# An expert layer's weight tiles in a new order, with the 32 extra tokens multiplied over two up-matrices at once

## The reference

```python
# x: 256 tokens x 1024. 8 experts, hidden size 3584, top 2 experts for each token
logits = h @ w_router + b_router            # 256 x 8
gate   = softmax over each token's 2 best experts
for e in experts:
    y += gate[:, e] * ((silu(h @ moe_w1[e]) * (h @ moe_w3[e])) @ moe_w2[e])
x = x + gt2 * y
```

## Time and profile before

| | us |
|---|---|
| median of 3 runs | 3112.54 (3109.74 to 3120.24) |
| the profiled execution's own time | 3107.25 |
| its span, first to last instruction | 3105.5 |
| PE busy in the span | 2710.2 (87%) |
| DVE busy | 1233.1 (40%) |
| ACT busy | 575.5 (19%) |
| mean granted clock of TensorE | 0.924 of full speed |

### The profile page before, as it was taken

One profiled execution on the slowest core, in us unless ns is written; L12 is line 12 of the kernel. 1 busy time (PEld: TensorE's weight loads), 2 busy tenths in 40 slices (PEclk: granted clock), 3 DMA queues, 4 the chain that ended last, 5 costly groups with the idle time before them and its releaser, 6 DMA issues.

```text
span 3105.5 us, 35726 instructions
## 1 busy us (share of the span) xinstructions
PE 2710.2 (87%) x14339; PEld 1731.7 (56%) x14339; DVE 1233.1 (40%) x1834; ACT 575.5 (19%) x905; POOL 281.0 (9%) x332
## 2 busy tenths in 40 slices
PE   5987999898678878879989989899899987668998
PEld 2754658754434434436767767574468653224883
DVE  2204235663401001006656656530245549981111
ACT  1101420001100000005535545400111010001110
POOL 1100410000000000000000000000000074650000
PEclk8997769999799999999989989999999997668999
DMA  7421728992399999997747657644258730003441
GB/s 282 97 80 53 205 82 300 324 338 100 112 394 394 394 395 393 394 396 268 256 172 255 221 201 259 218 136 149 81 190 293 275 135 28 0 0 115 149 150 67
DMA packets 315342, 648.45 MB, mean 209 GB/s; under 512 B 12450, under 2 KB 102765, under 8 KB 311040
## 3 DMA queue, kind: packets, MB, share of 16 engines
q10 hardware_dynamic: 151440, 358.68, 31.8%
q1 hardware_dynamic: 158544, 272.84, 25.5%
q0 software_dynamic: 5216, 14.96, 2.2%
HBM read 645.38 MB, written 1.05 MB: 208 GB/s over the span
## 4 chain that ended last, share of the span: by engine, by line
PE 64%; DMA 16%; DVE 12%; issue 3%; ACTq 2%; POOL 1%; ACT 1%; DVEq 0%; POOLq 0%
PE bank L1347 16%; DMA ring<-in_moe_w 11%; PE bank L1363 11%; PE bank L573 5%; PE bank L575 4%; PE bank L574 4%; PE bank L1589 4%; DMA arena<-in_w_ada 3%; PE bank L588 3%; DVE arena L1915 3%; ACTq L444 2%; PE bank L1675 2%; DVE arena L1924 2%; PE bank L533 1%; PE bank L585 1%
## 5 line engine op out<-in xcount | busy, mean ns | idle before, releaser
L1347 PE MATMUL bank<-HT,ring 128*128 128x256 f32 x2816 | 625.8, 386 | 19.0 <-DVE arena L1915 13.6
L1347 PEld LDWEIGHTS bank<-HT,ring 128*128 128x128 f32 x2816 | 544.8, 194 | 99.7 <-DVE arena L1915 15.7
L925 DVE TENSOR_TENSOR w_low<-ring,w_high 128x1024 fp32r<-128x1024 f32 x252 | 305.4, 1224 | 127.9 <-ACT w_high L731 125.7
L1363 PE MATMUL bank<-ring,arena 128*128 128x512 f32 x784 | 339.8, 595 | 0.7 <-ACT arena L1101 0.7
L731 ACT ACTIVATE w_high<-ring 128x1024 fp32r<-128x1024 f32 x252 | 265.3, 1059 | 195.4 <-PE bank L575 193.7
L1924 DVE SCALAR_TENSOR_TENSOR arena<-arena,small 128x512 f32<-128x512 f32 x288 | 216.6, 752 | 143.9 <-DMA arena<-in_ada_w 89.9
L1363 PEld LDWEIGHTS bank<-ring,arena 128*128 128x128 f32 x784 | 149.6, 191 | 188.4 <-issue 186.0
L909 DVE TENSOR_TENSOR HT<-HT,bank 128x256 f32<-128x256 f32 x35 | 14.7, 421 | 442.9 <-PE bank L547 425.4
L508 PE MATMUL bank<-ring,arena 128*64 128x256 f32 x1120 | 134.9, 384 | 45.0 <-DMA ring<-in_moe_w 45.0
L547 PE MATMUL bank<-ring,arena 128*64 128x256 f32 x1120 | 135.7, 385 | 43.0 <-DMA ring<-in_moe_w 42.9
L573 PE MATMUL bank<-w_high,tokens_low 128*128 128x512 f32 x336 | 144.1, 429 | 11.3 <-DVE w_low L925 8.5
(11 more groups left out here) (371 smaller groups left out, 3219.5 us busy)
## 6 DMA issues: line engine op xcount, KB each, us to landing
ring<-in_moe_w ACTq DMA_DIRECT2D x340, 1024.0 KB, 13.8
arena<-in_ada_w SPq DMA_DIRECT2D x96, 512.0 KB, 6.0
ring<-in_ffn_w_up SPq DMA_DIRECT2D x44, 1024.0 KB, 5.1
ring<-in_ffn_w SPq DMA_DIRECT2D x33, 1024.0 KB, 6.6
ring<-in_w_ada SPq DMA_DIRECT2D x24, 1024.0 KB, 9.8
arena<-in_w_ada SPq DMA_DIRECT2D x48, 512.0 KB, 5.5
ring<-in_ret_w_in SPq DMA_DIRECT2D x24, 1024.0 KB, 5.2
ring<-in_ffn_w_down SPq DMA_DIRECT2D x22, 1024.0 KB, 5.0
```

Of the source, the lines that this page charges most:

```text
L925: dve.tensor_tensor(out=WL[half % SPLIT][:, :], in0=slot(i)[:, HALF * (half % 2):HALF * (half % 2) + HALF], in1=WH[half % SPLIT][:, :], op ...
L1347: mm = pe.matmul(PS[b][:, SEQ * m:SEQ * m + SEQ], w[:, k, P * m:P * m + P], src[:, k, :], start=k == 0, stop=k == KD - 1)
L1363: mm = pe.matmul(bank(4 + 2 * t + n), lhs(2 * j + k)[:, P * t:P * t + P], w[:, k, BANK * n:BANK * n + BANK], start=j + k == 0, stop=j == t ...
```

## The change

The order of tiles becomes: in step c the tiles w1 h = 0, w3 h = 0, w1 h = 1, w3 h = 1 of chunk c, then both w2 tiles of chunk c - 1; 8 steps in place of 9. AHEAD is 3 in place of 4. PE, ACT and DVE follow that order. The extras of w1 and w3 are done together, once for each h, when both tiles are in the ring: column groups 0 and 1 take w1, groups 2 and 3 take w3, 256 columns each, all into bank 1. Silu of the extras is taken from partitions 0 to 63 and multiplied by partitions 64 to 127. The transposes of chunk c - 1 (4, then 2 of 64 partitions for the extras, before: 1 and 4) stand after the h = 0 part of chunk c. Before step c PE waits for the hidden values of chunk c - 1 (`moe_hid`), since banks 0, 1 and 2 are used again.

```diff
-MOE_STEPS = MOE_CHUNKS + 2
+MOE_STEPS = MOE_CHUNKS + 1
...
-        for name, chunk in (("w1", c), ("w2", c - 2), ("w3", c)):
-            if 0 <= chunk < MOE_CHUNKS:
-                order += [(name, chunk, 0), (name, chunk, 1)]
+        if c < MOE_CHUNKS:
+            order += [(name, c, h) for h in range(2) for name in ("w1", "w3")]
+        if c >= 1:
+            order += [("w2", c - 1, 0), ("w2", c - 1, 1)]
...
-        AHEAD = 4
+        AHEAD = 3
...
+                def extra_up(c, h):
+
+                    w = [cols_of(moe_first + tile_at[kind, c, h], 4) for kind in ("w1", "w3")]
+                    for k in range(4):
                         for n in range(4):
+                            mm = pe.matmul(PS[1][32 * n:32 * n + 32, 0:SEQ], XGX[:, 4 * h + k, :], w[n // 2][:, k, SEQ * (n % 2):SEQ * (n % 2) + SEQ],
+                                           start=h + k == 0, stop=h == 1 and k == 3)
+                    mm.then_inc(sem("tile_used"), 2)
...
+                    for q in range(4):
+                        pe.transpose(PS[7][:, P * q:P * q + P], MS[c % 2][:, P * q:P * q + P], ident[:, :])
+                    for b in range(2):
+                        mm = pe.transpose(PS[3][:, P + 64 * b:P + 64 * b + 64], MSX[c % 2][0:64, P * b:P * b + P], ident[0:64, 0:64])
+                    mm.then_inc(sem("moe_turned"), 1)
...
-                pe.wait_ge(sem("extra_x"), j + 1)
                 for c in range(MOE_STEPS):
+                    if c >= 1:
+                        pe.wait_ge(sem("moe_hid"), g * MOE_CHUNKS + c)
                     if c < MOE_CHUNKS:
-                        if c:
-                            pe.wait_ge(sem("moe_silu"), g * MOE_CHUNKS + c)
-                        tiles("w1", c, 0, 1)
+                        for h in range(2):
+                            for kind, b in (("w1", 0), ("w3", 2)):
+                                product(kind, c, 2 * h, b)
+                                product(kind, c, 2 * h + 1, b)
+                            if c + h == 0:
+                                pe.wait_ge(sem("extra_x"), j + 1)
+                            extra_up(c, h)
+                            if h == 0 and c >= 1:
+                                turn_hidden(c - 1)
                     if c == MOE_CHUNKS:
-                        pe.wait_ge(sem("moe_silu"), g * MOE_CHUNKS + MOE_CHUNKS)
+                        turn_hidden(c - 1)
                         pe.wait_ge(sem("pick_ready"), g + 2)
                         gather()
...
+                    if c >= 1:
+                        pe.wait_ge(sem("hid_low"), j * MOE_CHUNKS + c)
+                        if c == MOE_CHUNKS:
                             turn_gates()
+                        for h in range(2):
+                            product("w2", c - 1, 2 * h, 4)
+                            product("w2", c - 1, 2 * h + 1, 4)
+                            extra_down(c - 1, h)
```

On ACT in a wide round (DVE has the same order, with `hidden_low`, the two products into MS and MSX in place of `silu`, and `begin_round` after the first four halves of step 0):

```diff
                     if c < MOE_CHUNKS:
-                        split("w1", c)
...
+                        split("w1", c, 0, 2)
+                        split("w3", c, 0, 2)
+                        split("w1", c, 2, 4)
+                    if c >= 1:
+                        hidden_high(c - 1)
+                    if c < MOE_CHUNKS:
+                        split("w3", c, 2, 4)
+                    if c >= 1:
+                        split("w2", c - 1)
+                    if c < MOE_CHUNKS:
                         silu(c)
+                    else:
+                        act.wait_ge(sem("gather_done"), g + 2)
+                        tokens_high()
```

More of the change, by code:

```diff
@@ L380, in build @@
         MS = [hidden[:, BANK * i:BANK * (i + 1)] for i in range(2)]
-        MSX = [hidden[:, D + P * i:D + P * (i + 1)] for i in range(2)]
+        MSX = [hidden[:, D + SEQ * i:D + SEQ * (i + 1)] for i in range(2)]
         def in_ad(off, *shape):
@@ L500, in narrow @@
                         if c >= 2:
-                            pe.wait_ge(sem("moe_silu"), g * MOE_CHUNKS + (c - 1))
+                            pe.wait_ge(sem("moe_hid"), g * MOE_CHUNKS + (c - 1))
                         for h in range(2):
[L503 to L509, removed]
@@ L576, in product @@
                     mm.then_inc(sem("w_used"), 1)
-                def extra(kind, c, h, b):
-                    w = cols_of(moe_first + tile_at[kind, c, h], 2 if kind == "w2" else 4)
-                    for k in range(2 if kind == "w2" else 4):
+                def extra_up(c, h):
+                    w = [cols_of(moe_first + tile_at[kind, c, h], 4) for kind in ("w1", "w3")]
+                    for k in range(4):
                         for n in range(4):
[L583 to L589, removed]
-                    mm.then_inc(sem("tile_used"), 1)
@@ new lines, in extra_down @@
+                def extra_down(c, h):
+                    w = cols_of(moe_first + tile_at["w2", c, h], 2)
+                    for k in range(2):
+                        o = 64 * k + 32 * h
+                        for n in range(4):
+                            mm = pe.matmul(PS[6][32 * n:32 * n + 32, 0:SEQ], MHTX[c % 2][:, o:o + 32], w[:, k, SEQ * n:SEQ * n + SEQ],
+                                           start=c + h + k == 0, stop=c == MOE_CHUNKS - 1 and h + k == 2)
+                    mm.then_inc(sem("tile_used"), 1)
@@ L693, in narrow, with loads @@
                 now, after = experts_of(g)
+                def loads(first, used):
+                    for i in range(first, min(used + RING - AHEAD + 1, NT)):
+                        load_ahead(g, now, after, i)
+                    return max(first, used + RING - AHEAD + 1)
                 i = 0
                 for c in range(MOE_STEPS):
-                    until = tile_at["w1", c, 1] if c < MOE_CHUNKS else tile_at["w3", MOE_CHUNKS - 1, 1]
-                    while i <= until + RING - AHEAD:
-                        load_ahead(g, now, after, i)
-                        i += 1
+                    i = loads(i, tile_at["w3", c, 0] if c < MOE_CHUNKS else tile_at["w2", MOE_CHUNKS - 2, 1])
+                    if c >= 1:
+                        act.wait_ge(sem("moe_turned"), g * MOE_CHUNKS + c)
+                        if c >= 3:
+                            tile_wait(act, g, tile_at["w2", c - 3, 1])
+                        o = SEQ * ((c - 1) % 2)
+                        act.activation(MHTN[(c - 1) % 2], PS[7][:, o:o + SEQ].rearrange("p (b n) -> p b n", b=2), ACT.Copy)\
+                            .then_inc(sem("hid_turned"), 1)
                     if c < MOE_CHUNKS:
+                        i = loads(i, tile_at["w1", c, 1])
                         tile_wait(act, g, tile_at["w1", c, 1])
@@ L707, in narrow @@
                         tokens_high()
[L708 to L717 removed]
+                loads(i, NT - 1)
             def wide(g, j):
```

169 lines of the change are left out of this document (65 added, 104 removed).

## The result

| | before | after |
|---|---|---|
| median of 20 runs, us | 3110.53 (3103.72 to 3126.35) | 3125.70 (3116.03 to 3139.72) |
| ratio | | 1.0048, interval 1.0033 to 1.0062 |
| profiled execution, span, us | 3105.5 | 3137.3 |
| PE busy | 2710.2 | 2730.2 |
| PE instructions | 14339 | 13016 |

The change makes the kernel 0.48% slower, about 15 us. Fewer PE instructions and more time: the page's first lines already say that the loss is in waits or in slower matmuls.

The account below looks back on a forecast made before the run. It took DMA to bound the narrow rounds and PE, or waits made by the new order, the wide ones. Its terms summed to +6.5 us, which put on the median of 3112.54 gave 3119.0 us, range 3105 to 3130.

Parts of the forecast that it names:

- no change that can be told: Whole kernel: a difference under about 0.3% (9 us) either way, chance 0.50.
- AHEAD, first narrow round: Start of the narrow rounds: one preloaded tile fewer is one tile more to load afterwards, +2.3 us.
- end of the last narrow round: Last narrow round: two w2 tiles come at the DMA's pace before transposes, gather and two more w2 tiles, +1.8 us.
- merged extras, 42 pairs: Wide rounds: one extra group per pair of w1 and w3 tiles saves 0.37 us a pair, -15.5 us.
- old wait of step 1: Step 1 of each wide round: PE's old wait for hidden_high before w3 goes, -3.8 us.
- new gap, steps 0 to 1: Wide rounds: PE waits 2.8 us for moe_hid of chunk 0 and the next splits, +8.4 us for three rounds.
- wait behind the turn, 18: Steps 1 to 6 of the wide rounds: PE waits 0.72 us for the third half tile after the transposes, +13.0 us.
- turn itself, 21: Transposes in wide rounds: one more costs 0.1 us; +0.3 us for the three seventh turns, otherwise counted in the wait.
- clock in the gap: Rival, start of step 1 in wide rounds: clock falls to half, +6.5 us more, total 3125.5 us; chance 0.23.
- The first rival: Wide rounds: both new waits vanish, -14.9 us, 3097.6 us, or the extras save more; together chance 0.17.
- The third: Rival: merged extras gain nothing (+22 us) or DMA runs 1% slower (+12), 3125 to 3135 us; chance 0.10.
- three signs of being wrong: Steady wide step not 24.3 to 24.6 us, narrow rounds not 111.7, or low clock in the midst of a wide round.

Follow-up runs that it names:

- e1: The changed kernel with AHEAD = 4 again, all else as changed; ratio to the kernel before 1.0049.
- b1: The kernel before with AHEAD = 3 as its only edit; ratio to the kernel before 1.0001.
- e9_four: Changed kernel, hidden copies later, first split of chunk 1 before the extras' silu, whole transposes, AHEAD = 4, earlier next_pick; median 3105.25 us, ratio 0.9973 to the kernel before.
- e6: The changed kernel with the extras' two transposes on all 128 partitions and 128 columns; ratio to the kernel before 1.0027.
- e2: The changed kernel with hidden_high and hidden_low one place later, behind all four h = 1 half tiles; ratio to the kernel before 1.0015.
- e8: The changed order of tiles with the old extras, old single transpose and old layout; ratio to the kernel before 1.0038.

## Why the prediction was right or wrong

The range held (3105 to 3130, measured 3125.7), and the sign of the sum, +6.5, was right; its size was less than half of the 15.2, so that "no change that can be told" at 0.50 was the wrong case and "slower" at 0.33 the right one. By its own steps:

| term | predicted | measured | from |
|---|---|---|---|
| AHEAD, first narrow round | +2.3 | +2.6 | first narrow product to the last w3 tile; e1 gives 2.6, b1 3.1 |
| end of the last narrow round | +1.8 | +1.6 | the rest of the 4.26 |
| merged extras, 42 pairs | -15.5 | -15.1 | 8.02 to 7.66 |
| old wait of step 1 | -3.8 | -3.8 | absent after |
| new gap, steps 0 to 1 | +8.4 | +9.5 | 5.01 instead of 1.85 from extras to product |
| wait behind the turn, 18 | +13.0 | +7.2 | 0.40 each |
| turn itself, 21 | +0.3 for 3, in the wait for 18 | +6.9 | 0.85 against 0.52 |
| clock in the gap | 0, a rival at 0.23 | +3.1 in the trace | 2 of 3 rounds at 1.54 |
| start of rounds, clock | not there | +1.4 | first product to first extras, the 12 products more taken off |

**The step that failed** is the weighing of the clock. I took the fall as the less likely outcome because dense work stood ahead of the gap, and the gap of 2.57 us without a fall as the nearer neighbour. That neighbour was no evidence: the same gap has a fall in 8 of 11 traces. And the gap came out at 3.1, not 2.8, where the fall is the rule, 13 of 15. The 0.3 us are in one link of the chain: from the start of the extras' silu to the start of the split the sum had 0.3 and the trace has 0.65 (1446.89 to 1447.54), because ACT first issues the load that belongs to the tile. Where no load stands between them, in 30 places of e1_ahead4 and e9_four, it is 0.26 to 0.27, as here in e9_four:

```profile
1478.10 0.37 ACT L743 ACTIVATE HT<-bank 64x256 f32<-64x256 f32 x1
1478.37 1.05 ACT L731 ACTIVATE w_high<-ring 128x1024 fp32r<-128x1024 f32 x1
```

The other links, 1.09 from split to subtraction and 1.27 from there to the product, came as forecast (1.09 and 1.25). The price of a fall was put at 2.2 each and measured 1.54; a run with three falls pays 4.6 us. The fall accounts for 3.1 of the 8.7 us by which the sum was short. The rest are the gap's length (1.1), turn and wait (0.8), the start of the rounds (1.4) and small terms, and 1.8 that I can't assign.

**The step that was right with wrong parts** is the turn. "One transpose more, 0.1" missed that the two new ones work on 64 partitions. The start of the third half tile, 4.05 us after the turn's start, came out to within 0.05 (4.05, and 4.00 in e6 with the shape of transpose that the sum assumed), because it was read off a place in the old trace with the same order of instructions; so the sum of turn and wait came out (14.1 against 13.3), and the steady step of 24.51 too. But who expects the wait to be 0.72 expects too much from an edit that removes it, as I did in e2.

**The first rival**, that the waits hide, fell; ACT and DVE had the time but not the order. **The third**, that the extras don't save what they should, fell too: 0.36 a pair. e8 shows it from the other side.

The rest of the difference, about 0.8 us in the wide rounds and 0.95 between them, I can't assign; the latter is within what untouched code shows. The 1.4 at the start of the rounds needs no cause in the change: from the first product to the first extras the eight traces with merged extras show 7.08 to 8.53 us for the same instructions, in sum 22.8 to 24.9 over three rounds, and the kernel before, made comparable, 23.2.

Part of it is luck. The clock's case had 3125.5 and the measured median is 3125.7, but the kernel before came out 2.0 us lower than the median the forecast was put on and the difference 2.2 larger than that case, and of the 6.5 it gave to the clock the trace shows 3.1. Of the prediction's three signs of being wrong two stayed away, the steady step (24.51) and the narrow rounds (111.7 in both kernels); the third, low clock in the midst of a wide round, came.

## What to carry to other kernels

An order in which a bank is used again with no other work in between makes a wait that lies on the longest chain through ACT and DVE, and a gap of some 3 us on PE is mostly paid twice, once in itself and once in the clock behind it; moving two instructions ahead of the late one, or filling the gap, takes the second price away. Look in the old trace for a place with the new order's sequence of instructions: here its distance carried over to within 0.05 us, where sums of single durations were off by 0.2 to 0.3. A gap that was followed by full clock in one trace is no evidence that it is short enough: look at the same gap in several executions. And read short waits in the starts of matmuls, not in their idle time.

## What the runs showed of the hardware that was not expected

- The clock falls after an idle gap of 3.08 to 3.17 us even in the midst of dense products, in 13 of 15 cases, and costs 1.54 us of the next 24 products; after 1.13 us in none of 9, and with the gap filled in none of 3. Around a gap of 2.57 us behind lighter work it fell in 8 of 11.
- Two transposes of 64 partitions and 64 columns between work on 128 cost more than two of 128 by 128: 0.85 against 0.62 us for the whole turn.
- The issue of a load on ACT between two of its instructions moves the second's start from 0.26 to 0.27 us behind the first's (30 places in e1 and e9) to 0.64 to 0.73 (9 places in the changed kernel, e1 and e9).
- Sixteen float32 matmuls of 256 columns in four column groups take 1.86 us from their start to the next instruction's (1457.24 to 1459.10), eight take 1.00, and sixteen of 128 columns 1.01: the columns count, not the number of matmuls.
